# Mixture-of-experts stage: four experts packed into three tiles of 128 rows, tokens as the stationary operand in pieces of 32 or 64 columns

## The chip, the cores and the metric

The kernel is one program on one core of a Trainium2 chip. The metric is the device time of one execution, in microseconds (us). Everything is in float32. The names used below: PE is TensorE (PEld its weight loads), DVE is VectorE, ACT is ScalarE, POOL is GpSimd, SP is SyncE, which here only issues transfers.

## What is computed

The program is one step of a decoder layer with two token mixers, followed by a mixture of experts. The change touches only the experts. Each of 1056 tokens (1024 of a prompt, 32 of a sample batch) chooses two of 32 experts, and every expert runs its tokens through a gated network of width 256:

```python
def run_block(args):
    tok_b, w_b, e = args
    xb = h_pad[tok_b]
    yb = (jax.nn.silu(xb @ we_gate[e]) * (xb @ we_up[e])) @ we_down[e]
    return yb * w_b[:, None].astype(yb.dtype)
```

Here x has 1024 columns, `we_gate[e]` and `we_up[e]` are 1024x256 (kept side by side as `we_gu`, 2048 KB an expert), and `we_down[e]` is 256x1024 (1024 KB an expert).

## The kernel before

The stages run one after another: attention (fox), the recurrent mixer, the mixing products, the output product with the routing, `stage_moe`, and `stage_final`. The routing stage ends with a table in memory (`expert_table`) that has, for every expert, a list of slots with the token's row, the row where its result goes, and its weight. Slots without a token hold a row number out of bounds, so that nothing is fetched for them. `stage_moe` takes the first R = 96 slots of each expert; only if an expert had more would the rounds of `more_rounds` run, and with these inputs they don't.

`stage_moe` goes expert by expert (`first_round`, n = 0 to 31; the middle 24 in a loop of six passes over four buffers). For one expert:

- POOL copies the expert's column of slots to a fixed place (`at_fixed_place`), and an indirect transfer gathers its rows of h into `hx` (96 rows of 1024). After the results are ready it copies again, and scatters them (`scatter`).
- PE turns the rows (`pe_turn`, 8 transposes into `moe_hp`), and ACT and DVE move one half each to `hT`, times the norm's gain.
- PE makes gate and up (`pe_gate_up`): for each of four blocks of 128 outputs and eight blocks of the inner dimension, the weight block (128x128) is the stationary operand, and the 96 tokens in `hT` are the moving one. The result stands with the outputs on the partitions. ACT applies Silu, and DVE multiplies, which gives `aT`.
- PE makes the result (`pe_down`): `aT` (128 by 96 tokens) is stationary, `wd` moves with 512 columns, into `moe_yp`, two halves by two blocks: 4 products. ACT and DVE scale one half each into `y`.

On PE the order is: gate and up of expert n, the transposes of expert n + 1, the result of expert n. SP loads the weights of expert n + 4 when the result of expert n is made; the buffers of the first two experts (EARLY = 2) are filled in the stage before. A float32 product is one instruction in the program; in the trace it is two passes, each a weight load (LDWEIGHTS) and a MATMUL record. A transpose is one pass. Each product carries the size of array tile that it asks for: 128 columns of the array where the stationary operand has more than 64, 64 where it has 33 to 64, and 32 where it has at most 32, at the position that the output's first partition gives. A transpose of the kind used here is made with all 128.

Of the kernel before, what the change touches and what calls it, by code (L numbers as in the profile page):

```python
# [12 lines left out]
P = 128  # L13
D = 1024
# [11 lines left out]
R = 96  # L26
# [2060 lines left out]
def stage_moe(e):  # L2087
# [3 lines left out]

    nc, a, sem = e.nc, e.a, e.sem
    NW = 4
    w_loaded, gathered, scattered = ([sem(f"moe_{n}{b}") for b in range(NW)] for n in ("w_loaded", "gathered", "scattered"))
    names = "ent_loaded more_loaded turned hT_act hT_dve made_gu silu acted made_y y_dve y_act zero go placed0 placed1"
    q = {n: sem(f"moe_{n}") for n in names.split()}
    with memory(e) as (sb, ps), nc.Block() as block:
# [12 lines left out]
        hp = ps("moe_hp", [P, 2, 512])  # L2110
        gu = [ps(f"moe_gu{b}", [P, 512]) for b in range(2)]
        yp = [ps(f"moe_yp{b}", [R, 2, 512]) for b in range(2)]
        gut = [g[:, 0:4 * R].rearrange("p (t n) -> p t n", t=4) for g in gu]
        hpt = hp[:, :, 0:KD // 2 * R].rearrange("p c (k n) -> p c k n", n=R)
        half = KD // 2

        def after(eng, s, v):

            if not isinstance(v, int) or v > 0:
                eng.wait_ge(s, v)  # L2120


        def load_weights(sp, u, ex):
            sp.dma_start(wgu[u], a["we_gu"][ds(ex, 1)].squeeze(0)).then_inc(w_loaded[u], 16)
            sp.dma_start(wd[u], a["we_down"][ds(ex, 1)].squeeze(0)).then_inc(w_loaded[u], 16)

        def go(pool):

            pool.sem_inc(q["go"], 1)

        def at_fixed_place(pool, n, u, c):


            if c:
                pool.wait_ge(q["y_dve"], n + 1)
                go(pool)
            pool.tensor_copy(place[:, u, c:c + 1], index(n, c)).then_inc(q[f"placed{c}"], 1)
            pool.wait_ge(q[f"placed{c}"], n + 1)
            go(pool)
            return place[:, u, c:c + 1]  # L2140

        def gather(pool, u, token):
            pool.indirect_dma_start(out=hx[:, u], out_offset=None, in_=e.h_d,
                                    in_offset=bass.IndirectOffsetOnAxis(ap=token, axis=0),
                                    bounds_check=NT - 1, oob_is_err=False).then_inc(gathered[u], 16)

        def scatter(pool, n, u, row):
            pool.wait_ge(q["y_dve"], n + 1)
            pool.wait_ge(q["y_act"], n + 1)
            go(pool)  # L2150
            pool.indirect_dma_start(out=e.y2_d, out_offset=bass.IndirectOffsetOnAxis(ap=row, axis=0),
                                    in_=y[:, u], in_offset=None, bounds_check=2 * NT - 1,
                                    oob_is_err=False).then_inc(scattered[u], 16)

        def pe_turn(pe, n, i, u):
            pe.wait_ge(gathered[u], 16 * (i + 1))
            after(pe, q["hT_act"], n)
# [329 lines left out]
```

## Time and profile before

| | us |
|---|---|
| median of 3 runs (2082.20 to 2083.85) | 2082.69 |
| the profiled execution, its own time | 2081.27 |
| its span, first to last instruction | 2079.6 |
| expert stage on PE, first transpose to the last copy out of PSUM | 1641.3 to 2019.6 |

The profiled execution is a run of its own; its time and the span differ by what lies around the instructions. Mean granted clock of TensorE over the span: 0.944 of full speed. In the views that follow, a matmul's length in a row holds its way through the array too, and the rows of one kind overlap, so how long one takes of the engine is read from the distance between starts.

### The profile page before, as it was taken

What the parts mean: (1) busy time and instruction counts of PE and PEld (TensorE: products, weight loads), DVE (VectorE), ACT (ScalarE), POOL (GpSimd) and SP (SyncE); (2) the same over time, 40 slices, a digit from 0 to 9 for tenths busy, and PEclk for the clock granted to TensorE, in tenths of its full rate; (3) what the DMA queues carried; (4) which work ended last, traced back from release to release, by engine and by line L of the source; (5) the groups of instructions that cost most, each with busy time, mean ns of one, the idle gap of its engine ahead of it and who ended that gap; (6) DMA issues with size and microseconds to landing.
All of it is one profiled execution on the core that took longest, in us unless ns stands there. A gap on an engine that the chain in (4) does not pass through costs nothing. (4 is left out here: it accounts for less than half of the span.)

```text
span 2079.6 us, 36716 instructions
## 1 busy us (share of the span) xinstructions
PE 1837.3 (88%) x15442; PEld 1251.6 (60%) x15442; DVE 757.4 (36%) x1549; ACT 408.3 (20%) x877; POOL 245.5 (12%) x296
## 2 busy tenths in 40 slices
PE   6999789979999699999999996986996499999980
PEld 4654455558888476666666663434553377777760
DVE  4101656514655433333333322893234011111116
ACT  3010444502333011111111111110101011111112
POOL 2000656500000000000000000000001312112110
PEclk9999999989999799999999997995998699999995
DMA  5502999841110110111101107313300588888826
GB/s 186 210 1 92 327 318 354 300 163 31 30 32 19 36 42 27 42 33 46 36 33 46 37 19 243 124 61 136 126 31 31 171 324 312 324 306 327 310 79 260
DMA packets 86626, 292.62 MB, mean 141 GB/s; under 512 B 18488, under 2 KB 28344, under 8 KB 75952
## 3 DMA queue, kind: packets, MB, share of 16 engines
q1 hardware_dynamic: 65632, 228.72, 30.7%
q0 software_dynamic: 19536, 56.49, 7.7%
q10 hardware_dynamic: 1312, 5.31, 0.8%
q8 instruction: 110, 1.80, 0.4%
q14 instruction: 36, 0.29, 0.0%
HBM read 254.44 MB, written 43.90 MB: 143 GB/s over the span
## 5 line engine op out<-in xcount | busy, mean ns | idle before, releaser
L1287 PE MATMUL gate_p<-rows,gate_w 128*128 128x352 f32 x768 | 284.8, 490 | 0.7 <-DMA gate_w<-in_w_in 0.7
L1041 PE MATMUL rw_pp<-rows,rw_w 128*128 128x264 f32 x896 | 205.9, 391 | 9.3 <-DMA rows<-xn_rows 9.3
L1041 PEld LDWEIGHTS rw_pp<-rows,rw_w 128*128 128x128 f32 x896 | 171.1, 192 | 42.4 <-issue 11.3
L1287 PEld LDWEIGHTS gate_p<-rows,gate_w 128*128 128x128 f32 x768 | 129.9, 190 | 54.6 <-issue 3.8
L1879 PE MATMUL x_p<-late 128*128 128x512 f32 (+1 forms) x288 | 129.9, 606 | 1.5 <-PEq L1602 1.5
L2170 PEld LDWEIGHTS moe_gu<-rows,wgu 128*128 128x128 f32 x1024 | 119.9, 196 | 9.0 <-issue 7.6
L2170 PEld LDWEIGHTS moe_gu<-rows,late 128*128 128x128 f32 x1024 | 116.9, 192 | 8.1 <-issue 8.1
L2170 PE MATMUL moe_gu<-rows,wgu 128*128 128x96 f32 x1024 | 119.7, 279 | 1.1 <-ACT rows L2193 1.1
L2170 PE MATMUL moe_gu<-rows,late 128*128 128x96 f32 x1024 | 116.5, 275 | 0.0
L1656 POOL MEMSET empty<- 128x1056 int32 x1 | 1.0, 977 | 842.8 <-POOLq L1198 842.8
L1513 DVE TENSOR_TENSOR tl<-tl,scan_zb 128x256 f32<-128x256 f32 x64 | 27.0, 421 | 195.7 <-PE scan_zb L1301 195.7
L1879 PEld LDWEIGHTS x_p<-late 128*128 128x128 f32 (+1 forms) x288 | 52.0, 185 | 67.2 <-issue 67.2
L2209 DVE TENSOR_TENSOR rows<-rows,moe_gu 128x192 f32<-128x192 f32 x32 | 11.3, 354 | 217.7 <-ACT rows L2199 217.7
L1445 ACT COPY ys<-scan_yp 128x256 f32<-128x256 f32 x80 | 29.8, 373 | 226.3 <-PE scan_yp L1301 226.3
L1301 PEld LDWEIGHTS scan_yp<-tl,ltm 64*64 64x64 f32 x1280 | 43.6, 134 | 39.8 <-DVE tt L1514 32.0
L850 DVE CUSTOM_DVE_ANT_0 fox_work<-fox_a,fox_work 128x1024 f32<-128x1024 f32 (+7 forms) x64 | 47.1, 754 | 48.7 <-PE fox_a L546 39.8
L2214 DVE TENSOR_SCALAR obT<-moe_yp,moe_ent 96x512 f32<-96x512 f32 x32 | 23.9, 747 | 108.7 <-PE moe_yp L2179 108.7
L2179 PE MATMUL moe_yp<-wd,rows 128*96 128x512 f32 x128 | 58.8, 602 | 3.4 <-DVE rows L2209 1.9
L2179 PE MATMUL moe_yp<-late,rows 128*96 128x512 f32 x128 | 58.8, 602 | 3.0 <-DVE rows L2209 0.8
L397 POOL DMA_INDIRECT rows<-in_cache_kT,page_index x34 | 37.3, 1098 | 195.0 <-PE fox_a L492 179.2
L1665 PE MATMUL mix_b<-rows,mix_wa 128*128 128x512 f32 x128 | 59.8, 622 | 0.0
L1301 PE MATMUL scan_yp<-tl,ltm 64*64 64x64 f32 x1280 | 53.8, 223 | 5.2 <-DVE tt L1514 2.1
(382 smaller groups left out, 2980.2 us busy)
## 6 DMA issues: line engine op xcount, KB each, us to landing
wgu<-in_we_gu SPq DMA_DIRECT2D x16, 2048.0 KB, 8.5
late<-in_we_gu SPq DMA_DIRECT2D x16, 2048.0 KB, 8.3
wd<-in_we_down SPq DMA_DIRECT2D x16, 1024.0 KB, 12.2
late<-in_we_down SPq DMA_DIRECT2D x16, 1024.0 KB, 12.0
rows<-in_cache_v SPq DMA_DIRECT2D x44, 256.0 KB, 4.4
gate_rows<-u_rw SPq DMA_DIRECT2D x60, 176.0 KB, 1.8
rows<-in_cache_kT SPq DMA_DIRECT2D x34, 256.0 KB, 4.6
mix_gate<-gate_rows SPq DMA_DIRECT2D x16, 528.0 KB
```

Source lines behind the costliest of these rows:

```text
L397: return pool.indirect_dma_start(out=out, out_offset=None, in_=source, in_offset=bass.IndirectOffsetOnAxis(ap=index[:, column:column + 1], ...
L850: dve.tensor_tensor_reduce(prob[:, u % 2, s, 0:n], score[s][:, 0:n], ckb[:, p % 2, s, 0:n], -0.125, 3.0e38, ALU.add, ALU.min, stat[:, u % ...
L1041: mm = pe.matmul(pp[u % 2][:, c, 0:QN], w[:, n % 2, k, :], e.xnT[:, k, at:at + QN], start=(k == 0), stop=(k == KD - 1))
L1287: mm = pe.matmul(out[:, 0:GATE_N], gw[:, j % 2, k, :], e.xnT[:, k, at], start=(k == 0), stop=(k == KD - 1))
L1301: mm = pe.matmul(out(p, hs), lhsT(p, hs), rhs(p, hs), start=start, stop=stop)
L1445: act.copy(ys[:], ypv).then_inc(q["kept_y"], 1)
L1513: dve.tensor_tensor(tl[:], tl[:], zp[:, :, 0, :], ALU.subtract)
L1665: mm = pe.matmul(banks[n % NBK][:], weights[:, k], src[:, k, at:at + HN], start=(k == 0), stop=(k == HP - 1))
L1879: mm = pe.matmul(xp[t % 2][0:n, c], e.mixedT[:, k, t * P:t * P + n], wo[:, k, c * 512:(c + 1) * 512], start=(k == 0), stop=(k == KD - 1))
L2170: mm = pe.matmul(gut[d][:, t], wgu[u][:, k, t * P:(t + 1) * P], hT[:, d, k], start=(k == 0), stop=(k == KD - 1))
L2179: mm = pe.matmul(yp[d][:, c], aT[:, d, k], wd[u][:, k, c * 512:(c + 1) * 512], start=(k == 0), stop=(k == 1))
L2214: dve.tensor_scalar(y[:, u, 512:D], yp[d][:, 1], weight, None, ALU.mult).then_inc(q["y_dve"], 1)
```

## The change

Four experts make a group, and their 4 times 96 = 384 slots stand in three tiles of 128 rows, so there are 24 tiles in place of 32 experts. `PIECES` says which columns of a tile belong to which of the group's experts: (first column, columns, expert). Tile 0 has 64 and 32 columns of expert 0 and 32 of expert 1; tile 1 has 64 of expert 1 and 64 of expert 2; tile 2 has 32 of expert 2, and 32 and 64 of expert 3.

In gate and up the operands change places: a piece's tokens (128 by 32 or 64) are now the stationary operand, and the expert's `wgu` moves with all 512 columns. The result stands with the tokens on the partitions, so that Silu and the multiplication give `act`, which PE must turn (`turn_act`, 2 transposes into `moe_ap`) and DVE copy to `aT` (`keep_turned`) before the result is made. The result too is made by pieces. On PE the products of a tile are cut into four parts of two inner blocks; between the parts stand the transposes of the former tile's `act`, the former tile's result, and the transposes of the next tile's rows. There is one `moe_yp` in place of two. All 24 tiles are written out, with no loop. POOL gathers 128 rows at a time straight by `moe_ent`, without copies, and SP fills `moe_ent` with six transfers in place of one and waits for `made_gu` and `made_y` apart, tile by tile. The rounds beyond 96 slots are rewritten as well, and don't run.

```diff
     nc, a, sem = e.nc, e.a, e.sem
-    NW = 4
+    NW, NG, TILES = 4, NE // 4, NE * R // P
+    PIECES = (((0, 64, 0), (64, 32, 0), (96, 32, 1)), ((0, 64, 1), (64, 64, 2)), ((0, 32, 2), (32, 32, 3), (64, 64, 3)))
...
-        ent = sb("moe_ent", [R, NE, 4], I32)
-        more_ent, place = sb("moe_more_ent", [R, 4], I32), sb("moe_place", [R, NW, 2], I32)
-        hx = e.late[0:R, NL * 6 * D:NL * 6 * D + NW * D].rearrange("p (u n) -> p u n", u=NW)
-        y = e.obT[:].rearrange("p h n -> p (h n)")[0:R, 0:NW * D].rearrange("p (u n) -> p u n", u=NW)
-        hT = e.beside_x1[:, 0:2 * KD * R].rearrange("p (d k n) -> p d k n", d=2, k=KD)
-        act_g, aT = (e.beside_x1[:, (2 * KD + 4 * x) * R:(2 * KD + 4 * x + 4) * R].rearrange("p (d k n) -> p d k n", d=2, k=2)
-                     for x in range(2))
+        ent, more_ent = sb("moe_ent", [P, TILES, 4], I32), sb("moe_more_ent", [R, 4], I32)
+        hx = e.late[:, NL * 6 * D:NL * 6 * D + NW * D].rearrange("p (u n) -> p u n", u=NW)
+        y = e.obT[:].rearrange("p h n -> p (h n)")[:, 0:NW * D].rearrange("p (u n) -> p u n", u=NW)
+        hT = e.beside_x1[:, 0:2 * D].rearrange("p (d k n) -> p d k n", d=2, k=KD)
+        act_g, act = (e.beside_x1[:, 2 * D + x * 2 * DE:2 * D + (x + 1) * 2 * DE].rearrange("p (d n) -> p d n", d=2)
+                      for x in range(2))
+        aT = sb("moe_aT", [P, 2, 2, P])
+        hp, yp = ps("moe_hp", [P, 2, 512]), ps("moe_yp", [P, 2, 512])
         gu = [ps(f"moe_gu{b}", [P, 512]) for b in range(2)]
-        yp = [ps(f"moe_yp{b}", [R, 2, 512]) for b in range(2)]
...
+        def turn_tokens(pe, src, n, done):
             for k in range(KD):
-                mm = pe.transpose(hpt[:, k // half, k % half], hx[:, u, k * P:(k + 1) * P], e.c("ident")[0:R, 0:R])
-            mm.then_inc(q["turned"], 1)
-
-        def pe_gate_up(pe, n, i, u, d):
-            after(pe, w_loaded[u], 32 * (i if u < EARLY else i + 1))
-            pe.wait_ge(q["hT_act"], n + 1)
-            pe.wait_ge(q["hT_dve"], n + 1)
-            after(pe, q["acted"], n - 1)
-            for t in range(4):
-                for k in range(KD):
-                    mm = pe.matmul(gut[d][:, t], wgu[u][:, k, t * P:(t + 1) * P], hT[:, d, k], start=(k == 0), stop=(k == KD - 1))
-            mm.then_inc(q["made_gu"], 1)
-
-        def pe_down(pe, n, u, d):
-            pe.wait_ge(q["acted"], n + 1)
-            after(pe, q["y_act"], n - 1)
-            after(pe, q["y_dve"], n - 1)
+                mm = pe.transpose(hp[:, k // half, k % half * P:k % half * P + n], src[0:n, k * P:(k + 1) * P], e.c("ident")[0:n, 0:n])
+            mm.then_inc(done, 1)
+
+        def gate_up(pe, d, pieces, k):
+            for at, n, u in pieces:
+                mm = pe.matmul(gu[d][at:at + n, :], hT[:, d, k, at:at + n], wgu[u][:, k, :], start=(k == 0), stop=(k == KD - 1))
+            return mm
+
+        def turn_act(pe, d, n, done):
+            for k in range(2):
+                mm = pe.transpose(ap[:, k * P:k * P + n], act[0:n, d, k * P:(k + 1) * P], e.c("ident")[0:n, 0:n])
+            mm.then_inc(done, 1)
+
+        def down(pe, d, pieces, done):
             for c in range(2):
                 for k in range(2):
-                    mm = pe.matmul(yp[d][:, c], aT[:, d, k], wd[u][:, k, c * 512:(c + 1) * 512], start=(k == 0), stop=(k == 1))
-            mm.then_inc(q["made_y"], 1)
...
+                    for at, n, u in pieces:
+                        mm = pe.matmul(yp[at:at + n, c], aT[:, d, k, at:at + n], wd[u][:, k, c * 512:(c + 1) * 512],
+                                       start=(k == 0), stop=(k == 1))
+            mm.then_inc(done, 1)
...
+            table = e.table_d.rearrange("(g x c) k -> c x g k", x=4, c=e.CAP)
+            by_group = ent[:].rearrange("p (g i) k -> p g i k", i=3)
+            for i, at, n, x, first in ((0, 0, R, 0, 0), (0, 96, 32, 1, 0), (1, 0, 64, 1, 32), (1, 64, 64, 2, 0), (2, 0, 32, 2, 64),
+                                       (2, 32, R, 3, 0)):
+                sp.dma_start(by_group[at:at + n, :, i, :], table[first:first + n, x]).then_inc(ent_loaded, 16)
...
+            for g in range(1, NG):
+                t = 3 * (g - 1)
+                for u in range(2):
+                    sp.wait_ge(made_gu, t + u + 1)
+                    load_gate_up(sp, u, 4 * g + u)
+                    sp.wait_ge(made_y, t + u + 1)
+                    load_down(sp, u, 4 * g + u)
+                sp.wait_ge(made_gu, t + 3)
+                for u in range(2, 4):
+                    load_gate_up(sp, u, 4 * g + u)
+                sp.wait_ge(made_y, t + 3)
+                for u in range(2, 4):
+                    load_down(sp, u, 4 * g + u)
+
...
+            pool.wait_ge(ent_loaded, 16 * 6)
+            for t in range(NW):
+                gather(pool, hx[:, t], ent[:, t, 0:1], gathered[t])
+            for t in range(TILES):
+                if t + NW < TILES:
+                    pool.wait_ge(turned, t + 1)
+                    gather(pool, hx[:, t % NW], ent[:, t + NW, 0:1], gathered[t % NW])
+                pool.wait_ge(y_act, t + 1)
+                pool.wait_ge(y_dve, t + 1)
+                scatter(pool, y[:, t % NW], ent[:, t, 1:2], scattered[t % NW])
...
-            pe_turn(pe, 0, 0, 0)
-
-            def first(n, i, u, d):
-                pe_gate_up(pe, n, i, u, d)
-                if not isinstance(n, int) or n + 1 < NE:
-                    pe_turn(pe, n + 1, i + (u + 1) // NW, (u + 1) % NW)
-                pe_down(pe, n, u, d)
-            first_round(pe, first)
...
+            def products(t, ks):
+                for k in ks:
+                    if k == 0:
+                        pe.wait_ge(hT_act, t + 1)
+                        pe.wait_ge(hT_dve, t + 1)
+                        after(pe, acted, t - 1)
+                        for u in sorted({u for _, _, u in PIECES[t % 3]}):
+                            after(pe, gu_loaded[u], 16 * (t // 3 + (u >= EARLY)))
+                    mm = gate_up(pe, t % 2, PIECES[t % 3], k)
+                    if k == KD - 1:
+                        mm.then_inc(made_gu, 1)
+
+            def turned_act(t):
+                pe.wait_ge(acted, t + 1)
+                after(pe, aT_ready, t)
+                turn_act(pe, t % 2, P, a_turned)
+
+            def result(t):
+                pe.wait_ge(aT_ready, t + 1)
+                after(pe, y_act, t)
+                after(pe, y_dve, t)
+                for u in sorted({u for _, _, u in PIECES[t % 3]}):
+                    after(pe, wd_loaded[u], 16 * (t // 3 + (u >= EARLY)))
+                down(pe, t % 2, PIECES[t % 3], made_y)
+
+            turn(0)
+            for t in range(TILES):
+                products(t, (0, 1))
+                if t:
+                    turned_act(t - 1)
+                products(t, (2, 3))
+                if t:
+                    result(t - 1)
+                products(t, (4, 5))
+                if t + 1 < TILES:
+                    turn(t + 1)
+                products(t, (6, 7))
+            turned_act(TILES - 1)
+            result(TILES - 1)
...
+            def keep_turned(t):
+                dve.wait_ge(a_turned, t + 1)
+                after(dve, made_y, t - 1)
+                dve.tensor_copy(aT[:, t % 2], ap[:, 0:2 * P].rearrange("p (k n) -> p k n", k=2)).then_inc(aT_ready, 1)
...
+                dve.wait_ge(silu, t + 1)
+                after(dve, a_turned, t - 1)
+                dve.tensor_tensor(act[:, t % 2], act_g[:, t % 2], gu[t % 2][:, DE:2 * DE], ALU.mult).then_inc(acted, 1)
```

How the instructions stand on PE. Before, in the middle of the stage (`moe_gu` is gate and up, `moe_hp` the turned rows, `moe_yp` the result; `wgu` and `wd` are the early buffers, and `late` holds the other two), two experts are:

```order
L2179 MATMUL moe_yp<-wd,rows 96x512 x4
L2170 MATMUL moe_gu<-rows,late 128x96 x32
L2160 MATMUL moe_hp<-const,late 128x96 x8
L2179 MATMUL moe_yp<-late,rows 96x512 x4
L2170 MATMUL moe_gu<-rows,late 128x96 x32
L2160 MATMUL moe_hp<-const,late 128x96 x8
L2179 MATMUL moe_yp<-late,rows 96x512 x4
```

Now, in tile 0 of the second group, from the end of the second inner block (k = 1) through the turned `act` of the former tile (`moe_ap`) to the first products of the former tile's result, there stands:

```order
L2147 MATMUL moe_gu<-wgu,rows 32x512 x2
L2152 MATMUL moe_ap<-const,rows 128x128 x2
L2147 MATMUL moe_gu<-wgu,rows 64x512
L2147 MATMUL moe_gu<-wgu,rows 32x512 x2
L2147 MATMUL moe_gu<-wgu,rows 64x512
L2147 MATMUL moe_gu<-wgu,rows 32x512 x2
L2159 MATMUL moe_yp<-late,moe_aT 32x512 x2
L2159 MATMUL moe_yp<-late,moe_aT 64x512
L2159 MATMUL moe_yp<-late,moe_aT 32x512 x2
L2159 MATMUL moe_yp<-late,moe_aT 64x512
L2159 MATMUL moe_yp<-late,moe_aT 32x512 x2
L2159 MATMUL moe_yp<-late,moe_aT 64x512
```

What was one row of 32 products with full 128 columns of the array is now a row of one 64-column piece and a row of two 32-column pieces in turn, at each inner block; the result of a tile 2 is cut the same way.

And in tile 1 of that group, from k = 0 up to the first products of tile 0's result:

```order
L2147 MATMUL moe_gu<-wgu,rows 64x512
L2147 MATMUL moe_gu<-late,rows 64x512
L2147 MATMUL moe_gu<-wgu,rows 64x512
L2147 MATMUL moe_gu<-late,rows 64x512
L2152 MATMUL moe_ap<-const,rows 128x128 x2
L2147 MATMUL moe_gu<-wgu,rows 64x512
L2147 MATMUL moe_gu<-late,rows 64x512
L2147 MATMUL moe_gu<-wgu,rows 64x512
L2147 MATMUL moe_gu<-late,rows 64x512
L2159 MATMUL moe_yp<-wd,moe_aT 64x512
```

Here both pieces have 64 columns, one in each half of the array, and the full-width transposes stand between the second and the third block.

On POOL, at the start of the stage, before (`moe_place` is the fixed place):

```order
L2256 MEMSET late 96x4096
L2137 COPY moe_place<-moe_ent 96x1
L2143 DMA late<-h_rows,moe_place 96x1024
L2137 COPY moe_place<-moe_ent 96x1
L2143 DMA late<-h_rows,moe_place 96x1024
```

and now:

```order
L2218 MEMSET late 128x4096
L2133 DMA late<-h_rows,moe_ent 128x1024 x5
L2137 DMA y<-obT,moe_ent 2112x1024
L2133 DMA late<-h_rows,moe_ent 128x1024
L2137 DMA y<-obT,moe_ent 2112x1024
```

The copies are gone, and the gathers follow the clearing of `hx` directly; the fifth of them waits for the first tile to be turned.

## Rows read from the trace of the kernel before

**Rows 1.** The page: span and busy time of TensorE over the whole program.

```profile
span 2079.6 us, 36716 instructions
PE 1837.3 (88%) x15442; PEld 1251.6 (60%) x15442; DVE 757.4 (36%) x1549; ACT 408.3 (20%) x877; POOL 245.5 (12%) x296
```

**Rows 2.** Windows view; columns: stretch, its length, busy time of each engine, granted clock, DMA share, GB/s.

```profile
core 0: us, PE busy (x) PEld busy (x) DVE busy (x) ACT busy (x) POOL busy (x), PEclk, DMA share, GB/s
1700.00:1950.00 250.00, 245.75 (x1706) 195.41 (x1706) 34.35 (x65) 44.46 (x131) 48.45 (x84) 1.00 0.87 318
```

**Rows 3.** Timeline of one expert; columns: start, length, engine, line, operation, tiles, shapes, count.

```profile
1658.80 7.28 PE L2170 MATMUL moe_gu<-rows,wgu 128*128 128x96 f32 x64
1665.92 0.83 PE L2160 MATMUL moe_hp<-const,late 96*128 96x96 f32 x8
1666.89 3.67 PE L2179 MATMUL moe_yp<-wd,rows 128*96 128x512 f32 x8
1655.80 0.16 PEld L2179 LDWEIGHTS moe_yp<-wd,rows 128*96 128x96 f32 x1 [0.27 <-issue]
...
1658.37 0.19 PEld L2170 LDWEIGHTS moe_gu<-rows,wgu 128*128 128x128 f32 x1 [0.27 <-issue]
```

**Rows 4.** Tile view of moe_ent: the copies of the upper half of y out of PSUM.

```profile
L2214 DVE TENSOR_SCALAR obT<-moe_yp,moe_ent x32: 745/747/749, 1659.0 to 2019.6; 96x512 f32<-96x512 f32 x32
```

**Rows 5.** Timeline of TensorE in the attention stage, 300 to 318 us.

```profile
300.83 0.38 PE L602 MATMUL fox_b<-const,dec_prob 128*128 128x128 f32 x2
301.14 1.92 PE L654 MATMUL fox_b<-rows,dec_probT 128*32 128x512 f32 x16
303.00 1.53 PE L581 MATMUL fox_b<-fox_work,v_tok 128*64 128x128 f32 x24
304.46 0.55 PE L556 MATMUL fox_b<-const,fox_work 128*128 128x128 f32 x3
303.00 0.53 PEld L581 LDWEIGHTS fox_b<-fox_work,v_tok 128*64 128x64 f32 x10 [0.84 <-issue]
```

**Rows 6.** Windows view of a stretch of the attention stage.

```profile
224.00:274.00 50.00, 45.80 (x576) 28.50 (x574) 29.63 (x95) 25.68 (x61) 34.10 (x32) 1.00 0.96 354
```

**Rows 7.** DMA issues of the page: the loads of one expert, and their time to landing.

```profile
wgu<-in_we_gu SPq DMA_DIRECT2D x16, 2048.0 KB, 8.5
wd<-in_we_down SPq DMA_DIRECT2D x16, 1024.0 KB, 12.2
```

**Rows 8.** Timeline at the start of the expert stage.

```profile
1627.91 0.33 SPq L2241 DMA_DIRECT2D moe_ent<-expert_table  x1
1627.93 3.51 POOL L2256 MEMSET late<- 96x4096 f32 x1 [4.33 <-POOLq L180]
...
1631.50 0.18 POOL L2137 COPY moe_place<-moe_ent 96x1 int32<-96x1 int32 x1
1632.64 1.02 POOL L2143 DMA_INDIRECT late<-h_rows,moe_place  x1 [0.95 <-POOL moe_place L2137]
...
1641.28 1.54 PE L2160 MATMUL moe_hp<-const,late 96*128 96x96 f32 x8 [31.45 <-DMA late<-h_rows,moe_place]
...
1643.95 10.53 PE L2170 MATMUL moe_gu<-rows,wgu 128*128 128x96 f32 x64 [1.13 <-ACT rows L2193]
```

**Rows 9.** Timeline at the end of the expert stage.

```profile
2015.16 0.33 ACT L2199 ACTIVATE rows<-moe_gu 128x192 f32<-128x192 f32 x1 [6.43 <-PE moe_gu L2170]
2015.53 0.35 DVE L2209 TENSOR_TENSOR rows<-rows,moe_gu 128x192 f32<-128x192 f32 x1 [6.73 <-ACT rows L2199]
...
2015.93 3.67 PE L2179 MATMUL moe_yp<-late,rows 128*96 128x512 f32 x8 [0.81 <-DVE rows L2209]
2019.64 0.69 ACT L2204 ACTIVATE obT<-moe_yp,moe_ent 96x512 f32<-96x512 f32 x1 [4.15 <-PE moe_yp L2179]
...
2020.56 0.18 POOL L2137 COPY moe_place<-moe_ent 96x1 int32<-96x1 int32 x1 [9.50 <-DVE obT L2214]
2021.73 0.93 POOL L2151 DMA_INDIRECT y<-obT,moe_place  x1 [0.99 <-POOL moe_place L2137]
```

More of the change, by code:

```diff
@@ L2142, in gather @@
[L2142 to L2153, printed above, removed]
@@ L2259, in _ @@
-            for u in range(NW):
-                gather(pool, u, at_fixed_place(pool, u, u, 0))
-            def first(n, i, u, d):
-                if not isinstance(n, int) or n + NW < NE:
-                    pool.wait_ge(q["turned"], n + 1)
-                    go(pool)
-                    gather(pool, u, at_fixed_place(pool, n + NW, u, 0))
-                scatter(pool, n, u, at_fixed_place(pool, n, u, 1))
-            first_round(pool, first)
-            for u in range(NW):
-                pool.wait_ge(scattered[u], 16 * (NE // NW))
@@ new lines, in _, with low, out, body @@
+            more_rounds(pe, body)
+        @block.scalar
+        def _(act_e):
+            def low(t):
+                act_e.wait_ge(turned, t + 1)
+                after(act_e, made_gu, t - 1)
+                low_half(act_e, t % 2, P, hT_act)
+            def out(t):
+                act_e.wait_ge(made_y, t + 1)
+                after(act_e, scattered[t % NW], 16 * (t // NW))
+                act_e.activation(y[:, t % NW, 0:512], yp[:, 0], ACT.Copy, scale=weight(t)).then_inc(y_act, 1)
+            low(0)
+            for t in range(TILES):
+                if t:
+                    out(t - 1)
+                if t + 1 < TILES:
+                    low(t + 1)
+                act_e.wait_ge(made_gu, t + 1)
+                after(act_e, acted, t - 1)
+                act_e.activation(act_g[:, t % 2], gu[t % 2][:, 0:DE], ACT.Silu).then_inc(silu, 1)
+            out(TILES - 1)
+            def body(m, ex, r):
+                act_e.wait_ge(more["turned"], m + 1)
+                low_half(act_e, 0, R, more["hT_act"])
+                act_e.wait_ge(more["made_gu"], m + 1)
+                act_e.activation(act_g[0:R, 0], gu[0][0:R, 0:DE], ACT.Silu).then_inc(more["silu"], 1)
+                act_e.wait_ge(more["made_y"], m + 1)
+                act_e.activation(y[0:R, 0, 0:512], yp[0:R, 0], ACT.Copy, scale=more_weight).then_inc(more["y_act"], 1)
+            more_rounds(act_e, body)
@@ L2332, in _, with high, out @@
-            more_rounds(dve, more)
+            def high(t):
+                dve.wait_ge(turned, t + 1)
+                after(dve, made_gu, t - 1)
+                high_half(dve, t % 2, P, hT_dve)
+            def keep_turned(t):
+                dve.wait_ge(a_turned, t + 1)
+                after(dve, made_y, t - 1)
+                dve.tensor_copy(aT[:, t % 2], ap[:, 0:2 * P].rearrange("p (k n) -> p k n", k=2)).then_inc(aT_ready, 1)
+            def out(t):
+                dve.wait_ge(made_y, t + 1)
+                after(dve, scattered[t % NW], 16 * (t // NW))
+                dve.tensor_scalar(y[:, t % NW, 512:D], yp[:, 1], weight(t), None, ALU.mult).then_inc(y_dve, 1)
```

204 lines of the change are left out of this document (90 added, 114 removed).

## The prediction, made before the changed kernel ran

> **What bounds the kernel now.** I read the page first: TensorE (PE) is busy 88% of the span [rows 1]. That is a mean over stages, so I then read the windows of the stage that is changed. From 1700 to 1950 us PE is busy 245.75 of 250 us at a granted clock of 1.00, and the DMA engines have a share of 0.87 [rows 2]: PE sets the pace, and the transfers come second, not far off. The copies of y out of PSUM start 32 times from 1659.0 to 2019.6 us [rows 4], so an expert takes 360.6 / 31 = 11.63 us. Its weights land 8.5 and 12.2 us after issue [rows 7], just inside four buffers' time.
>
> The timeline shows what the 11.63 us hold [rows 3]. Gate and up are 64 passes (two for each of 32 products), from 1658.80 to the transposes at 1665.92: 7.12 us, 0.111 each. The eight transposes are one pass each; the 0.97 us up to the result, at 1666.89, hold them and a wait for DVE. The weight loads of the result lie six steps apart between 1655.80 and 1658.37: a pass of 512 columns takes 0.428 us (0.429 in long rows), eight take 3.43. So a column costs 0.84 ns in a pass of 512, while the gate-and-up passes of 96 columns cost 1.16 ns a column: their 128-column weight loads, not their columns, set the pace. There is something to gain there, 64 times (0.111 - 0.080) = 2.0 us an expert at most, if columns alone counted.
>
> **What the change does to PE.** Every product now moves 512 columns, so every pass takes 0.429 us, and all depends on how many pieces run at once. The attention stage has such products. Sixteen passes with 32 stationary columns and 512 moving ones start at 301.14, and the next line starts at 303.00 [rows 5]: 1.86 us for 16, where one after another they would take 6.9. Four pieces, each with its own moving operand, run side by side in four parts of the array. The 24 passes with 64 columns behind them take 303.00 to 304.46, 1.46 us, which is 12 times 0.109 (a quarter of 0.429 and a little) and 0.15 over: two side by side. That stretch ran at clock 1.00 with a DMA share of 0.96 [rows 6], so neither the second moving stream nor busy transfers spoil it.
>
> *Passes.* At one inner block, tile 1 needs 2 pass times (its two 64-column pieces side by side). Tiles 0 and 2 have one 64-column piece and two 32-column ones. If only pieces of one width run together, they need 2 + 2. A group of three tiles then has 8 x (4 + 2 + 4) = 80 pass times in gate and up and 4 x (4 + 2 + 4) = 40 in the result: 120 x 0.429 = 51.5 us, and 30 transposes of 128 columns at 0.109 are 3.3: 54.8 us, where four experts took 46.5. Eight groups: 438 us. At three seams of each group but the first, pieces of one width in different parts follow each other and overlap (the last 32-column pieces of k = 3 with the first of the former tile's result, that result's last 64-column piece with k = 4, and tile 2's last with tile 0's first): 21 x 0.858 = 18 us less, 420.
>
> *Changes of width.* The row at 300.83 has two passes of 128 columns, 0.22 us, so the next line could start at 301.05; it starts at 301.14. The 16 passes of width 32 hold 4 x 0.429 = 1.72 of their 1.86 us, and 0.144 is over; the 64-wide ones have 0.15 over [rows 5]. Between full-width lines there is nothing of the kind: the load at 1658.37 is issued 0.43 us ahead of its product at 1658.80 [rows 3], but the loads of the 64-wide line start at 303.00, together with its first product. So at a change of width the engine holds even the weight loads until all before has ended; it pays a gap of about 0.09 us and the first load. I take 0.125 us for a stretch of width 32 (two pieces to start, not four) and 0.147 for one of 64 or 128. Along the written order I counted 434 changes, 185 into width 32 and 249 into the others (transposes count as 128): 23.1 + 36.6 = 59.7 us. Ends of this price: 0.09 for each (the gap alone), 39 us, and 0.15 for each, 65 us.
>
> Whether a 64-column piece runs beside a 32-column one in other columns, no row shows: wherever the width changes in this trace the columns collide too. From below, all side by side, PE's work would be 274 us; from above it is 480. I take the upper one, for loads that touch no column in use are held as well. The Trainium skill, TensorEngine Tiling (Array Packing), section Key Properties, says the same outright: changing the tiling mode, and not just the tile, drains TensorE. By that rule the sum is the 480 us; rows bear out the gap, not yet the lost overlap.
>
> *The sum.* Before, from the first gate and up at 1643.95 to the copy at 2019.64, it was 375.7 us [rows 8, 9]. Now: 479.7, less 0.9 for the first transposes, which lie ahead of that start; plus 3.3, because the first 64 passes took 10.53 us against 7.28 at the lower clock (1.2 GHz) and the clock rises no sooner now; plus 2.0 at the end, where 2015.16 to 2015.93 (silu, multiplication, and 0.8 us of PE waiting) gets transposes and a DVE copy on top. 484.1, or 108.4 us more.
>
> *What is hidden, and the ends.* Silu, the multiplication, the turned act and its copy take some 1 us between two parts of products of at least 1.7 us; were that cover gone, each tile would wait up to 0.5 us, 12 us in all. A new tile's hT must be ready when the fourth part ends, 1.7 us after the transposes; the one before took 1.1 (1641.28 + 1.54 to 1643.95, [rows 8]). The single moe_yp must be copied (0.75, [rows 4]) before the next result, some 10 us later. The weights need 34 to 40 us of DMA a group, and a group lasts 59: SP's waits cost nothing. At the start [rows 8] SP issues six transfers for moe_ent at 0.33 to 0.45 us each in place of one, so they land some 2 us later and the four weight loads queued behind them go out as much later, not needed before tile 1; the copy before the first gather, 1.1 us, is gone: +1 us, with ends of -2 and +8 (the gather took 8.6 us from 1632.64 to 1641.28 behind the weights). At the end the scatter needs no copy (2020.56 to 2021.73): -1.1 us. Sum: 108.3 us. The profiled execution took 2081.27 us, 1.4 below the median 2082.69; on the median that is **2191 us**.
>
> **Rivals.** *All pieces side by side, whatever their width: faster.* For it: four pieces with four streams do run together [rows 5]. Against it: the held loads. PE would need 274 / 8 = 34 us a group; then the DMA engines are the bound, 0.87 x 11.63 = 10.1 us an expert, 324 us for 32, less 17 for the two loaded before and more for idle moments: some 325 against 375.7, 2030 us. It decides once a group takes less than 46.5 us. The same page's Overview gives up to 2x for 64 columns and 4x for 32, with no word of a mix; taken alone, that is this case.
>
> *Widths alternate pass by pass.* Two passes of each product are written in a row, yet four products' first passes run together, so the engine takes passes out of the written order. Did it do so across widths, the 24 mixed steps of a group would have four changes in place of two: 48 x 0.136 x 8 = 52 us more, 2243.
>
> *A change of width costs nothing, but pieces of two widths don't overlap:* 60 us less, 2131. Against it: every change in [rows 5].
>
> *No overlap at all:* 192 pass times a group in place of 120, less seams: 265 us more, 2456. Against it: the four pieces of [rows 5].
>
> **How the numbers follow.** The forecast has 0.78, side by side 0.10, alternating widths 0.04, free changes 0.03, no overlap 0.02, anything else (PE waiting for hT or transfers, a lower clock) 0.03. The forecast's own range: the low price of a change takes 21 us off and the start 3 (2167); the high one adds 5, lost cover 12, the start 7 (2215). Widened a little for the unnamed: 2160 to 2220, which holds about 8 in 10 without the far cases. Faster by over 0.2% (4 us, about what a measurement tells from no change) is the side-by-side case, 0.11; within it 0.01; slower 0.88.
>
> **What will show it.** A PE timeline of a tile 0: at each inner block about 0.98 us for the 64-wide piece and about 0.98 for the two others, 0.27 of the two for changes. Tiles 0, 1, 2 some 22.3, 18.8 and 18.6 us apart by their token transposes, a group 59.6; PE without idle time; a DMA share near 0.68 (0.87 x 46.5 / 59.6); the loads landing well ahead. A start of the 32-wide pieces within 0.1 us of the 64-wide one would make it wrong, as would PE idle behind ACT, DVE or a load.

## The result and the profile after

The changed kernel takes 2190.3 us (median of 4 runs, 2189.41 to 2191.86), the kernel before 2082.44 beside it: a ratio of 1.052, with an interval of 1.0506 to 1.0534. The forecast was 2191. On another chip, later, the ratio was 1.0511 (1.0496 to 1.0525).

The page of the changed kernel, its span and TensorE's row, answering to [rows 1], and further down the loads of one expert, answering to [rows 7]:

```profile
span 2189.5 us, 34438 instructions
PE 1949.4 (89%) x14658; PEld 1067.1 (49%) x14658; DVE 761.1 (35%) x1549; ACT 395.7 (18%) x829; POOL 221.0 (10%) x216
...
wgu<-in_we_gu SPq DMA_DIRECT2D x16, 2048.0 KB, 8.8
late<-in_we_gu SPq DMA_DIRECT2D x16, 2048.0 KB, 10.3
wd<-in_we_down SPq DMA_DIRECT2D x16, 1024.0 KB, 4.9
```

PE is busy 112 us longer and the span is 109.9 us longer (2189.5 less 2079.6): the loss is on PE. The windows view of the stage, and of one group of three tiles, says how (columns as in [rows 2]):

```profile
1700.00:2100.00 400.00, 400.00 (x1491) 93.03 (x1490) 45.78 (x80) 44.33 (x120) 38.10 (x38) 1.00 0.65 241
1720.00:1779.60 59.60, 59.60 (x224) 13.88 (x222) 6.87 (x12) 6.65 (x18) 6.08 (x6) 1.00 0.67 249
```

PE is busy all of the time, at full clock, and does less in it: 1491 passes in 400 us, where it did 1706 in 250. The DMA share fell from 0.87 to 0.65. Nothing waits for a load.

What fills the time stands in the weight loads. This is the timeline of PEld in the last inner blocks of a tile 0 ahead of the next tile's transposes (`moe_hp`):

```profile
1720.09 0.14 PEld L2147 LDWEIGHTS moe_gu<-wgu,rows 128*32 128x32 f32 x4 [0.81 <-issue]
1721.07 0.19 PEld L2147 LDWEIGHTS moe_gu<-wgu,rows 128*64 128x64 f32 x2 [0.84 <-issue]
1722.07 0.14 PEld L2147 LDWEIGHTS moe_gu<-wgu,rows 128*32 128x32 f32 x4 [0.81 <-issue]
1723.05 0.86 PEld L2142 LDWEIGHTS moe_hp<-const,late 128*128 128x128 f32 x8 [0.84 <-issue]
1724.08 0.19 PEld L2147 LDWEIGHTS moe_gu<-wgu,rows 128*64 128x64 f32 x2 [0.17 <-issue]
```

Each row of `moe_gu` is one width at one inner block. The 64-column piece (1721.07) starts 0.98 us after the two of 32, and these again 1.00 after it: two passes of 0.429, a gap and a first load each time, with no load pulled ahead. One inner block costs 1.98 us; side by side it would be 0.86.

In a tile 1, where both pieces have 64 columns, they do run side by side. Timeline of PE:

```profile
2098.49 0.59 PE L2147 MATMUL moe_gu<-wgu,rows 128*64 128x512 f32 x1
2098.50 0.59 PE L2147 MATMUL moe_gu<-late,rows 128*64 128x512 f32 x1
2098.92 0.59 PE L2147 MATMUL moe_gu<-wgu,rows 128*64 128x512 f32 x1
```

The two pieces start 0.01 us apart, and the next pass of the first comes 0.43 us later. So the lost overlap is between widths, not between pieces.

The start of the stage, timeline, answering to [rows 8]:

```profile
1629.05 3.48 SPq L2191 DMA_DIRECT2D moe_ent<-expert_table  x6
1629.07 3.51 POOL L2218 MEMSET late<- 128x4096 f32 x1 [4.34 <-POOLq L180]
...
1634.95 1.05 POOL L2133 DMA_INDIRECT late<-h_rows,moe_ent  x1 [2.37 <-DMA moe_ent<-expert_table]
...
1646.22 1.97 PE L2142 MATMUL moe_hp<-const,late 128*128 128x128 f32 x8 [35.27 <-DMA late<-h_rows,moe_ent]
...
1649.42 14.10 PE L2147 MATMUL moe_gu<-wgu,rows 128*64 128x512 f32 x36 [1.23 <-ACT rows L2165]
```

The end, timeline, answering to [rows 9]:

```profile
2123.02 0.44 PE L2152 MATMUL moe_ap<-const,rows 128*128 128x128 f32 x2 [0.93 <-DVE rows L2367]
2123.50 0.42 DVE L2351 COPY moe_aT<-moe_ap 128x256 f32<-128x256 f32 x1 [0.53 <-PE moe_ap L2152]
2123.98 8.01 PE L2159 MATMUL moe_yp<-late,moe_aT 128*32 128x512 f32 x24 [0.52 <-DVE moe_aT L2351]
2132.03 0.69 ACT L2319 ACTIVATE obT<-moe_yp,moe_ent 128x512 f32<-128x512 f32 x1 [9.51 <-PE moe_yp L2159]
...
2133.61 0.98 POOL L2137 DMA_INDIRECT y<-obT,moe_ent  x1 [16.85 <-DVE obT L2356]
```

From the first gate and up (1649.42) to the last copy out of PSUM (2132.03) it is 482.6 us, against 375.7 before: 106.9 more.

### The profile page after: what moved, and what is told of

Its sections match the earlier page's. It is cut to its first block and busy times, and to the rows that moved or that the text cites. A ratio compares the mean times of both kernels' runs of the same rounds, so it can differ in the third digit from the quotient of the medians.

```text
span 2189.5 us, 34438 instructions
## 1 busy us (share of the span) xinstructions
PE 1949.4 (89%) x14658; PEld 1067.1 (49%) x14658; DVE 761.1 (35%) x1549; ACT 395.7 (18%) x829; POOL 221.0 (10%) x216
## 5 line engine op out<-in xcount | busy, mean ns | idle before, releaser
L2147 PE MATMUL moe_gu<-wgu,rows 128*32 128x512 f32 (+1 forms) x512 | 192.5, 614 | 1.2 <-ACT rows L2165 1.2
L1041 PEld LDWEIGHTS rw_pp<-rows,rw_w 128*128 128x128 f32 x896 | 170.5, 191 | 42.5 <-issue 11.4
L2147 PE MATMUL moe_gu<-late,rows 128*64 128x512 f32 (+1 forms) x512 | 190.4, 608 | 0.0
L2147 PEld LDWEIGHTS moe_gu<-wgu,rows 128*32 128x32 f32 (+1 forms) x512 | 36.6, 122 | 120.8 <-issue 119.2
L2159 PE MATMUL moe_yp<-late,moe_aT 128*64 128x512 f32 (+1 forms) x256 | 92.8, 605 | 0.5 <-DVE moe_aT L2351 0.5
L2159 PE MATMUL moe_yp<-wd,moe_aT 128*64 128x512 f32 (+1 forms) x256 | 92.8, 605 | 0.0
L2356 DVE TENSOR_SCALAR obT<-moe_yp,moe_ent 128x512 f32<-128x512 f32 x24 | 18.0, 751 | 211.5 <-PE moe_yp L2159 211.5
L2147 PEld LDWEIGHTS moe_gu<-late,rows 128*64 128x64 f32 (+1 forms) x512 | 36.3, 121 | 95.9 <-issue 89.4
L2319 ACT ACTIVATE obT<-moe_yp,moe_ent 128x512 f32<-128x512 f32 x24 | 16.5, 687 | 289.7 <-PE moe_yp L2159 289.7
L2137 POOL DMA_INDIRECT y<-obT,moe_ent x24 | 24.2, 1007 | 435.3 <-DVE obT L2356 435.3
L2142 PE MATMUL moe_hp<-const,late 128*128 128x128 f32 x192 | 27.1, 286 | 35.3 <-DMA late<-h_rows,moe_ent 35.3
```

What stands on the lines that cost most here:

```text
L1041: mm = pe.matmul(pp[u % 2][:, c, 0:QN], w[:, n % 2, k, :], e.xnT[:, k, at:at + QN], start=(k == 0), stop=(k == KD - 1))
L2142: mm = pe.transpose(hp[:, k // half, k % half * P:k % half * P + n], src[0:n, k * P:(k + 1) * P], e.c("ident")[0:n, 0:n])
L2147: mm = pe.matmul(gu[d][at:at + n, :], hT[:, d, k, at:at + n], wgu[u][:, k, :], start=(k == 0), stop=(k == KD - 1))
L2159: mm = pe.matmul(yp[at:at + n, c], aT[:, d, k, at:at + n], wd[u][:, k, c * 512:(c + 1) * 512], start=(k == 0), stop=(k == 1))
```

## The experiments

My theory (A) was that TensorE does not run pieces of 64 and of 32 columns side by side, and that each change of width costs some 0.14 us beside. The rivals: the swap of operands itself is what costs, or the packing, or the interleaving. Chips differ in the stages ahead of the experts (the kernel before took 2119.5 us on the chip of four of the runs, 2083 to 2085 on the others, and the expert stage began at 1663 us in the first run below, at 1629 in the changed kernel's trace), so I compare differences to the kernel before on the same chip.

### One width: all pieces of 32 columns

```diff
-    PIECES = (((0, 64, 0), (64, 32, 0), (96, 32, 1)), ((0, 64, 1), (64, 64, 2)), ((0, 32, 2), (32, 32, 3), (64, 64, 3)))
+    PIECES = tuple(tuple((32 * q, 32, u) for q, u in enumerate(us)) for us in ((0, 0, 0, 1), (1, 1, 2, 2), (2, 3, 3, 3)))
```

> The changed kernel with every 64-column piece cut into two of 32, nothing else: same packing, same interleaving, same transfers. Theory A (what the extra 108 us are: 64-column and 32-column pieces never run side by side, and each change of width costs some 0.14 us): with one width only transposes change it, PE's own work falls from 480 to 287 us (35.9 a group), and the DMA engines become the bound at some 40 a group: 2030 to 2045 us in all, PE idle for loads; if transfers were no bound, 1997. Rival B (the swap of the operands itself is what costs, 512 moving columns in each pass): no more than the 434 less 95 changes come back, about 47 us: 2143.

2038.26 us against 2119.52: 81.3 less than the kernel before, a ratio of 0.962 (0.9593 to 0.9647). The change of one line turns a loss of 108 us into a gain. The windows view of the stage:

```profile
1720.00:1950.00 230.00, 227.46 (x2006) 75.04 (x2009) 43.23 (x76) 42.12 (x114) 36.40 (x36) 1.00 1.00 406
```

2006 passes in 230 us, 8.7 a microsecond, against 3.7 in the changed kernel. Most tiles stand 11.97 us apart, 35.9 a group against 59.6. The 23.7 us less can be added up: the 42 changes of width that are gone make 5.8 (at 0.137), and the 42 pass times that now run beside others (48 with a mix, less six at the seams) 18.0. Theory A's 35.9 holds; rival B, which would have given back 47 us, is out. My bound by the DMA engines was wrong, though: I had put 2030 to 2045 us for a chip where the kernel before takes 2082, that is, at most 52 less; it was 81. The loads ran at 406 GB/s at a share of 1.00, and PE waited 2.5 us for them in five places between 1700 and 1970 us.

### The same pieces, ordered by width

```diff
+            for same in by_width(pieces):
+                for k in ks:
+                    for at, n, u in same:
+                        mm = pe.matmul(gu[d][at:at + n, :], hT[:, d, k, at:at + n], wgu[u][:, k, :], ...)
```

> The changed kernel with the order of the pieces turned: within each part of two inner blocks, and within each result, all pieces of one width come first, then those of the other. The passes and what can overlap stay; changes of width fall from 434 to 210. Theory A: 224 changes less at about 0.135 us, 30 us less than the changed kernel: 2160. Rival (a change is free, the loss is all in the missing overlap): 2190. Rival (the price is on the loads pulled ahead, 0.43 a change): 2094.

2180.82 us, 61.3 above the kernel before, where the changed kernel is 107 above: 46 less, more than my 30 and far from 0 and 96. A group takes 17.87 + 17.68 + 17.80 = 53.35 us by its transposes, 6.25 less than 59.60. The 28 changes saved make 3.8 us of it. The timeline of PE in a tile 0 has the rest:

```profile
1797.16 2.48 PE L2156 MATMUL moe_gu<-wgu,rows 128*64 128x512 f32 x6
1799.05 0.62 PE L2169 MATMUL moe_yp<-late,moe_aT 128*32 128x512 f32 x2
1799.48 0.60 PE L2156 MATMUL moe_gu<-wgu,rows 128*32 128x512 f32 x2
1799.50 0.60 PE L2169 MATMUL moe_yp<-late,moe_aT 128*32 128x512 f32 x2
1799.91 0.60 PE L2156 MATMUL moe_gu<-wgu,rows 128*32 128x512 f32 x2
1799.93 0.60 PE L2169 MATMUL moe_yp<-late,moe_aT 128*32 128x512 f32 x2
```

The first two 32-column products of the result (`moe_yp`, L2169, written after two inner blocks of gate and up) start at 1799.05, beside the first block's, and the two lines go on in step: a seam of one width overlaps with all that stands ready on either side, here two products deep and not one. At three seams a group that is 2 more pass times each, 6 x 0.429 = 2.6 us. 3.8 + 2.6 = 6.4 against 6.25. That split is worked out, not measured apart; it agrees with the 0.12 to 0.14 us that each change takes in the rows of PEld above. So the price of a change stands, and the seams give more than I knew.

### The interleaving undone

```diff
-                products(t, (0, 1))
-                if t:
-                    turned_act(t - 1)
-                products(t, (2, 3))
-                if t:
-                    result(t - 1)
-                products(t, (4, 5))
+                products(t, range(KD))
                 if t + 1 < TILES:
                     turn(t + 1)
-                products(t, (6, 7))
-            turned_act(TILES - 1)
-            result(TILES - 1)
+                turned_act(t)
+                result(t)
```

> The changed kernel with its interleaving undone: all products of a tile, then the next tile's transposes, the turned act, the result. Theory A: PE's own work goes from 480 to 489 us (fewer seams where pieces of one width overlap, fewer changes by transposes), and each tile now waits about 0.3 us for silu and the multiplication and 0.7 us for the copy of the turned act, 24 us in all: 2224. Rival (the cover was not needed, the chains hide elsewhere): 2200. Rival (the interleaving is itself what costs): below 2190.

2334.12 us: 214.6 above the kernel before, where I had expected 142. The waits are longer than I had worked out, and they bring something else. The timeline of one tile:

```profile
1752.05 1.09 PE L2142 MATMUL moe_hp<-const,late 128*128 128x128 f32 x8
1753.18 1.15 ACT L2165 ACTIVATE rows<-moe_hp,vec 128x128 f32<-128x128 f32 x4 [16.20 <-PE moe_hp L2142]
1754.20 0.40 ACT L2322 ACTIVATE rows<-moe_gu 128x256 f32<-128x256 f32 x1
1754.63 0.42 DVE L2360 TENSOR_TENSOR rows<-rows,moe_gu 128x256 f32<-128x256 f32 x1 [0.76 <-ACT rows L2322]
1755.11 0.64 PE L2152 MATMUL moe_ap<-const,rows 128*128 128x128 f32 x2 [1.97 <-DVE rows L2360]
1756.26 7.72 PE L2159 MATMUL moe_yp<-late,moe_aT 128*32 128x512 f32 x16 [0.52 <-DVE moe_aT L2344]
```

ACT makes the next tile's hT (1753.18) before this tile's silu, since they stand in that order in its queue, so PE is idle 1.97 us and then 0.52. And behind the wait 16 passes take 7.72 us. The windows view of those 12 us gives the reason, a granted clock of 0.72, between full speed (2.4 GHz) and half of it (1.2). Its second line is the whole stage:

```profile
1750.00:1762.00 12.00, 9.52 (x28) 2.24 (x28) 1.54 (x3) 1.42 (x5) 0.00 (x0) 0.72 0.75 296
1690.00:2270.00 580.00, 519.98 (x1762) 117.18 (x1760) 53.47 (x94) 50.34 (x140) 42.40 (x42) 0.94 0.48 179
```

The same two waits stand behind all tiles but the first and the last (the first has a longer one), yet not every tile loses the clock, though the expectation of the next run says so: behind them it was 1.00 from 1830 to 1842 us and from 1930 to 1942, and 0.86 from 1785 to 1797. What decides it in one tile and not in another stays open.

### Silu and multiplication ahead of the next hT

The same kernel; in ACT's and DVE's queues the silu and the multiplication of tile t now stand ahead of `low(t + 1)` and `high(t + 1)`.

```diff
-                if t + 1 < TILES:
-                    low(t + 1)
                 act_e.wait_ge(made_gu, t + 1)
                 act_e.activation(act_g[:, t % 2], gu[t % 2][:, 0:DE], ACT.Silu).then_inc(silu, 1)
+                if t + 1 < TILES:
+                    low(t + 1)
```

> The run without interleaving again, with one thing turned: ACT and DVE do the silu and the multiplication of a tile before the next tile's hT, not behind it. In the run without interleaving PE stood idle 1.97 us and 0.52 us in every tile and then worked at half the clock for 7 us, and it came out 215 us above the kernel before, where I had expected 142. Theory C (the length of the idle stretch is what lost the clock, and the clock is the rest of the loss): the first wait shrinks to 0.1 to 0.3 us, the second stays at 0.5 to 0.9, the granted clock stays at 1.00 in the stage, and the kernel lies 130 to 150 us above the kernel before. Rival D (the clock falls with any wait of this kind, or the loss lies elsewhere): 190 us or more above.

2221.82 us, 139.0 above the kernel before (ratio 1.0673, 1.0653 to 1.0694). The waits view of PE, 1700 to 2150 us, and the windows:

```profile
PE moe_yp L2159 <- DVE moe_aT L2344: 16.0, 21, 0.8
```

```profile
1780.00:2100.00 320.00, 308.54 (x1116) 71.64 (x1114) 32.98 (x61) 33.25 (x91) 29.34 (x29) 1.00 0.62 231
```

One wait of 0.8 us is left a tile, the clock is 1.00, and 76 us are back. PE idles some 40 us less in the stage than without the turn (46.7 + 11.9 us there in 23 tiles); the rest, some 35, is what a mean clock of 0.94 in place of 1.00 over 580 us comes to. Theory C holds for the time, D is out.

### The swap without the packing

One expert a tile of 96 rows, in three pieces of 32 columns; 32 tiles; one table load; the rest as in the changed kernel.

```diff
-    NW, NG, TILES = 4, NE // 4, NE * R // P
-    PIECES = (((0, 64, 0), (64, 32, 0), (96, 32, 1)), ((0, 64, 1), (64, 64, 2)), ((0, 32, 2), (32, 32, 3), (64, 64, 3)))
+    NW, NG, TILES = 4, NE // 4, NE
+    PIECES = tuple(tuple((32 * q, 32, u) for q in range(3)) for u in range(4))
```

> The operands swapped as in the changed kernel, but no packing: one expert a tile of 96 rows, in three pieces of 32 columns, 32 tiles, interleaved in the same way, one table load as before, the loads of one expert's weights as its gate and up, and its result, are made. Theory A: an expert costs PE 24 passes of 0.429, ten transposes and four changes of width, 11.68 us, against 11.63 before: 374 us, and as one table load does, 2080 to 2086 us, the same as before. Rival B (the swap itself costs): 2140 or more. So with the run of one width and packing, it says what the packing alone is worth.

2123.73 us against 2119.52, a ratio of 1.0021. This kernel also had one wait in the routing stage changed; the next one is the same without that:

> The run with one expert a tile of 96 rows in three pieces of 32 columns, once more: in its first form one wait of the routing stage had been changed too, by a slip (on the second load of x, tile 3), which is put right here. Expected the same result, 0 to 0.4% above the kernel before, since that wait lies 80 us and more ahead of the expert stage and cost nothing there.

2084.71 us against 2082.96: 1.0011 (1.0002 to 1.0020). The tiles stand 11.69 us apart (11.68 worked out, 11.63 before). So the swap by itself costs next to nothing here (0.1%, 0.2% at most): 24 passes of 0.429 with the fourth quarter of the array empty are what 64 passes of 0.111 and eight of 0.429 were. What the kernel with one width gains, it gains by filling that quarter.

The changed kernel stood beside it once more:

> The changed kernel itself again, on another chip and beside the run above, as the ground for differences to it: 4.9 to 5.4% above the kernel before, with tiles 22.25, 18.75 and 18.60 us apart as in its first trace.

2189.81 us, a ratio of 1.0511, and its tiles 22.25, 18.75 and 18.60 us apart, within 0.01.

### The first gather ahead of the weights

The kernel with pieces of 32, with its start changed:

```diff
-                sp.dma_start(by_group[at:at + n, :, i, :], table[first:first + n, x]).then_inc(ent_loaded, 16)
+                sp.dma_start(by_group[at:at + n, :, i, :], table[first:first + n, x]).then_inc(ent_first if i == 0 else ent_loaded, 16)
+            sp.wait_ge(gathered[0], 16)
             for u in range(EARLY, NW):
                 load_gate_up(sp, u, u)
...
-            pool.wait_ge(ent_loaded, 16 * 6)
+            pool.wait_ge(ent_first, 16 * 2)
```

> The run with all pieces of 32 columns, with its start changed: POOL's first gather waits for the first two table loads alone, not for six, and SP holds back the weight loads of experts 2 and 3 until that gather has landed. Theory A: the gather took 11 us in the changed kernel because 6 MB of weights went out beside it; alone it lands in 3 to 4 us, and the first tile starts 7 to 9 us earlier; the held weights are needed only 12 us later and take 6 us for the first of them. So 6 to 9 us less than the run with pieces of 32, 86 to 90 us below the kernel before. Rival (the time of a gather is its own, row by row, whatever runs beside it): no gain, or a loss by PE waiting for the held weights at tile 1.

1994.35 us, 88.5 below the kernel before (ratio 0.958, 0.9562 to 0.9597). The start, timeline:

```profile
1630.45 3.48 SPq L2192 DMA_DIRECT2D moe_ent<-expert_table  x6
...
1634.80 1.05 POOL L2134 DMA_INDIRECT late<-h_rows,moe_ent  x1 [0.82 <-POOL late L2220]
...
1638.85 0.82 SPq L2128 DMA_DIRECT2D late<-in_we_gu  x2
...
1638.88 1.97 PE L2143 MATMUL moe_hp<-const,late 128*128 128x128 f32 x8 [26.53 <-DMA late<-h_rows,moe_ent]
```

The gather lands 4.1 us after its issue, not 11.3, and from the first table load to the first transpose it is 8.4 us instead of 17.2. That a gather's time is its own is out: it is the weights beside it. In all it gives 7 us over the run with pieces of 32, though that difference is between two chips.

The 32 more rows of a gather are not what makes it slow. The run with one expert a tile (the second one) has one table load and gathers 96 rows, as before, and its first gather took 11.4 us (timeline):

```profile
1633.65 1.00 POOL L2133 DMA_INDIRECT late<-h_rows,moe_ent  x1 [0.86 <-POOL late L2207]
1645.05 1.54 PE L2142 MATMUL moe_hp<-const,late 96*128 96x96 f32 x8 [33.87 <-DMA late<-h_rows,moe_ent]
```

### The transposes together, and what holds them

```diff
-                products(t, (0, 1))
+                products(t, (0, 1, 2))
                 if t:
                     turned_act(t - 1)
-                products(t, (2, 3))
-                if t:
-                    result(t - 1)
-                products(t, (4, 5))
                 if t + 1 < TILES:
                     turn(t + 1)
-                products(t, (6, 7))
+                products(t, (3, 4))
+                if t:
+                    result(t - 1)
+                products(t, (5, 6, 7))
```

> The gather-first run, with PE's full-width transposes put together: three inner blocks, the turned act of the former tile and the transposes of the next tile's rows side by side, two blocks, the former result, three blocks. The changes of width fall from 95 to 51. Theory A by PE's own work: 44 less at 0.14, 6 us below the gather-first run. Rival (the DMA engines, at a share of 1.00 in the run with pieces of 32, now set the pace): within 2 us of the gather-first run, with PE idle before products for a load.

1993.55 us, 0.8 less than without: no difference that can be told. Tiles 1 and 2 come 11.68 us after each other (11.97 before), as the changes saved would have it, but a group's first tile comes late:

```profile
1891.14 4.34 PE L2148 MATMUL moe_gu<-wgu,rows 128*32 128x512 f32 x24 [2.32 <-DMA wgu<-in_we_gu]
```

Whether that is the amount moved or the moment at which buffers come free I asked with two kernels on one chip. The first leaves out the loads of the down weights after the first group and makes the later results with the first group's, so its output is not the reference's; the second is the kernel above again.

> The kernel with the transposes together, without the loads of the down weights after the first group: the results of the later groups are made with the first group's down weights, so the output is not the reference's; PE's work is the same, the stage moves a third less of weights. Theory A (in the transposes-together run PE idles 8 us before tile 0 of the groups, up to 2.3 us at once and then with a slower clock, because the DMA engines can't bring the next gate-and-up weights in time): the idle stretches before loads go, a group takes 35.0 us by PE alone, and the kernel comes out 8 to 13 us below the same kernel with all loads. Rival (what stands behind those waits is when the buffers come free, not how much is moved): the waits stay, within 3 us.

> The transposes-together kernel again, unchanged, on the chip of the run without down loads, as what that one is to be compared with. Expected 4.0 to 4.4% below the kernel before, as in its first run, with PE waiting for gate-and-up loads for some 8 us.

1983.21 us with fewer loads, 1993.42 with all: 10.2 less. The windows of the two, first without the down loads, then with:

```profile
1680.00:1920.00 240.00, 239.04 (x2170) 82.84 (x2162) 45.07 (x82) 43.10 (x122) 38.35 (x38) 1.00 0.71 281
```

```profile
1680.00:1920.00 240.00, 233.79 (x2106) 81.00 (x2102) 43.46 (x79) 42.18 (x120) 37.38 (x37) 0.99 0.97 398
```

Without them every tile stands 11.68 us apart and PE waits for no load; the buffers come free at the same point of a tile in both (SP issues a gate-and-up load 2.72 us ahead of the next transposes: 1721.03 and 1723.75 without, 1726.44 and 1729.16 with). So it is the amount moved: at 398 GB/s and a share of 0.97 the transfers take turns with PE as the bound, and what PE saves is given back before tile 0.

## Why the prediction was right, and where not

The direction, the size and the mechanism came out as forecast, but it is partly luck that 108.3 us forecast and 109.9 measured (on the spans) lie so close: the stage took 1.5 us less than its term and the start 3.3 more, the end gave 0.6 less, and two differences that the text does not have (+1.1 ahead of the stage, -2.0 behind it) stand beside them.

**The bound and the passes.** Right. The transposes stand 22.25, 18.75 and 18.60 us apart in every group behind the first, 59.60 a group; the text's terms give 59.7 (54.8, less three seams of 0.858, plus an eighth of 59.7 for the changes). The time of a pass and the price of a change came out of the rows of another stage [rows 5]. The clock and the DMA share of that stretch were read from a window that lies elsewhere, 224 to 274 us [rows 6]; a window of 300 to 318 us has the same clock, 1.00, and a share of 0.98, so nothing hangs on it. Nor does anything on the words that the loads land "just inside four buffers' time": 8.5 and 12.2 us are about the time of one expert, 11.63. Of the stage's 1.5 us, 1.2 lie at its start: the first two inner blocks took 6.1 us where two at full clock take 4.0, 2.1 more and not 3.3.

**The lost overlap**, which no row showed and which I took from the held weight loads. Right: the rows of a tile 0 show it (1.98 us for an inner block), and so does the run of one width, for nothing else changed in it; by the price of a change, 18.0 of the 23.7 us that a group gained are that overlap. The Trainium skill, TensorEngine Tiling (Array Packing), section Key Properties, says that a change of tiling mode drains TensorE; this case agrees, with 0.98 to 1.00 us for each width at each inner block and some 0.14 us of it for the change.

**Changes of width.** Right in size: 434 changes were put at 0.137 each on average, and the rows of PEld have 0.12 into width 32 and 0.14 into width 64. The run ordered by width gave 6.25 us a group, which 28 changes and six pass times at seams explain.

**The start.** The term was mis-sized: +1 us forecast with ends of -2 and +8. The first gate and up came 5.5 us later than before (1649.42 against 1643.95), 1.1 of it since the stage itself began later, so 4.3. The gather was issued 1.2 us later in the stage (5.90 us behind its start against 4.73), as forecast; that is the table loads less the copy. The miss is the time of the gather itself, 11.3 us where 8.6 was taken over from before, and 0.5 more from the gather to the first product, for 128 rows in place of 96, which the sum did not have. The text let the four weight loads go out later as if that cost nothing, yet it is behind them that the gather waits (4.1 us without them). Why 8.6 became 11.3 is not shown: it was 11.4 with 96 rows too, so the rows don't explain it; in both kernels the two gate-and-up loads go out first, and the gathers follow each other at 1.3 us in place of 2.1, and neither was tried by itself. The end gave 0.5 us back, not 1.1, and behind the last scatter the kernel is 2.0 us shorter, which I have not explained. Start, stage and end make 1.1 + 4.3 + 106.9 - 0.5 - 2.0 = 109.8, where the spans differ by 109.9.

**What is hidden.** Right that it is: the waits view of PE from 1660 to 2130 us has two waits, 0.9 and 0.5 us, both in the last tile. Wrong in what it would cost if the cover were gone: "each tile would wait up to 0.5 us, 12 us in all" was some 107 us (214.6 above the kernel before, where the changed kernel is 107 to 108). I left out what stands ahead of the silu in ACT's queue (the waits came to some 60 us) and the clock (some 35); the rest fits the 9 us more of PE's own work that the expectation had worked out for fewer seams.

**The rival of the other side.** Its mechanism, all side by side, is what the kernel of one width does; its price was too high by some 30 us, for I took a DMA share of 0.87 at 318 GB/s to mean that 366 were the most.

## What to carry to other kernels

Before pieces of the array are packed, look at which tile width each product asks for, and keep neighbours on PE at one width: it decides whether packing is worth 4% or costs 5%. What a product of such a kind costs can be read from another stage of the same trace, in distances between starts. And ask of a cover (work that stands between an instruction and what it needs, so that nothing waits) not only what would wait without it but also what TensorE's clock would do.

## What the runs showed of the hardware

Products in free columns start ahead of earlier written ones, two deep at least, as long as the width is the same (1799.05 in the run ordered by width); across a change of width nothing starts early, not even a weight load. The clock fell behind idle stretches of 1.97 and 0.52 us with two transposes between them in some tiles (0.72 over 12 us, and 16 passes in 7.72 us) and not in others, and did not with a single 0.8. With the transposes together it fell behind a single wait of 2.32 us (24 passes in 4.34 us, 0.62 from 1891.1 to 1895.4) and not behind one of 1.15 (24 passes in 2.78 us, 1.00). A DMA share is not a share of the bandwidth: 0.87 at 318 GB/s before, 0.91 at 317 with one expert a tile, 1.00 at 406 with one width.
